# Two SwiGLU networks in one kernel: the first chunk's product taken before the norm's roots are known

## What is computed

```python
def rms_norm(x, g, eps=NORM_EPS):
    xf = x.astype(jnp.float32)
    y = xf * lax.rsqrt(jnp.mean(xf * xf, axis=-1, keepdims=True) + eps)
    return (y * g.astype(jnp.float32)).astype(x.dtype)

def swiglu_ffn(h, norm, w13, w2):
    u = rms_norm(h, norm) @ w13
    return (jax.nn.silu(u[..., :FFN_HIDDEN]) * u[..., FFN_HIDDEN:]) @ w2
```

## Time and profile before

| | |
|---|---|
| median of 3 runs | 3366.26 us (3365.47 to 3368.86) |
| the profiled execution's own time | 3368.29 us |
| span of its trace | 3366.4 us |
| TensorE busy | 3304.4 us, 98% of the span |
| VectorE busy | 1763.8 us, 52% |
| GpSimd, ScalarE busy | 1492.0 us, 44%; 1435.9 us, 43% |
| granted TensorE clock, mean | 0.997 |

### The profile page before, as it was taken

One profiled execution on the slowest core, in us unless ns is written; L12 is line 12 of the kernel. 1 busy time (PEld: TensorE's weight loads), 2 busy tenths in 40 slices (PEclk: granted clock), 3 DMA queues, 4 the chain that ended last, 5 costly groups with the idle time before them and its releaser, 6 DMA issues. The chain is left out here.

```text
span 3366.4 us, 48377 instructions
## 1 busy us (share of the span) xinstructions
PE 3304.4 (98%) x19096; PEld 2724.3 (81%) x19096; DVE 1763.8 (52%) x3073; ACT 1435.9 (43%) x2918; POOL 1492.0 (44%) x1353
## 2 busy tenths in 40 slices
PE   9999999999998999999999999999999999999999
PEld 7769788888886788888888877888888877888887
DVE  4765675636456664656353376445153186545143
ACT  4662354323355554532333337344343246444343
POOL 3330254454443545354544443445554443444543
PEclk9999999999999999999999999999999999999999
DMA  4210024545221123354533220232323220123331
GB/s 124 75 57 4 27 88 151 194 144 192 85 88 51 42 97 100 101 169 163 170 125 117 82 77 11 75 100 86 102 85 103 92 82 26 51 89 99 100 94 56
DMA packets 233851, 317.79 MB, mean 94 GB/s; under 512 B 8877, under 2 KB 151196, under 8 KB 233628
## 3 DMA queue, kind: packets, MB, share of 16 engines
q1 hardware_dynamic: 204982, 260.50, 24.1%
q10 hardware_dynamic: 28646, 54.22, 4.7%
HBM read 312.59 MB, written 2.10 MB: 93 GB/s over the span
## 5 line engine op out<-in xcount | busy, mean ns | idle before, releaser
L417 PE MATMUL banks<-split,split 128*128 128x512 f32 (+2 forms) x11760 | 2675.2, 388 | 8.1 <-ACT split L436 3.7
L417 PEld LDWEIGHTS banks<-split,split 128*128 128x128 f32 x11760 | 2183.7, 188 | 476.5 <-issue 15.7
L440 POOL TENSOR_TENSOR split<-kept,split 128x512 fp32r<-128x512 f32 (+3 forms) x1174 | 1363.8, 1166 | 1581.1 <-ACT split L436 1578.6
L436 ACT ACTIVATE split<-kept 128x512 fp32r<-128x512 f32 (+3 forms) x1174 | 648.9, 559 | 1436.4 <-PE banks L417 1389.3
L2047 DVE SCALAR_TENSOR_TENSOR work<-banks,kept,work 128x511 f32<-128x511 f32 (+1 forms) x176 | 120.4, 745 | 257.1 <-ACT work L2029 256.3
L1044 DVE SCALAR_TENSOR_TENSOR work<-work,kept 128x512 f32<-128x512 f32 x168 | 195.5, 1164 | 6.0
L989 DVE SCALAR_TENSOR_TENSOR kept<-banks,kept 128x512 f32<-128x512 f32 (+1 forms) x56 | 34.3, 669 | 207.8 <-PE banks L417 207.8
L987 DVE TENSOR_TENSOR kept<-banks,kept 128x512 f32<-128x512 f32 (+1 forms) x72 | 41.1, 625 | 193.2 <-PE banks L417 193.2
L613 DVE COPY work<-banks 128x512 f32<-128x512 f32 (+1 forms) x64 | 37.4, 643 | 187.9 <-PE banks L417 187.9
L1986 DVE TENSOR_TENSOR work<-work,banks 128x512 f32<-128x512 f32 x44 | 28.3, 684 | 165.5 <-ACT work L1974 165.5
L1673 ACT ACTIVATE work<-work 128x128 f32<-128x128 f32 (+3 forms) x160 | 89.5, 560 | 47.0 <-DVE work L1733 46.1
(11 more groups left out here) (460 smaller groups left out, 3106.7 us busy)
## 6 DMA issues: line engine op xcount, KB each, us to landing
work<-in_mod_w ACTq DMA_DIRECT2D x48, 1024.0 KB, 6.5
kept<-in_ffn_w SPq DMA_DIRECT2D x94, 512.0 KB, 4.9
kept<-in_w_up SPq DMA_DIRECT2D x88, 512.0 KB, 4.7
kept<-in_w_in SPq DMA_DIRECT2D x36, 1024.0 KB, 5.0
kept<-in_od_w_in SPq DMA_DIRECT2D x19, 1024.0 KB, 5.2
kept<-in_ffn_w SPq DMA_DIRECT2D x18, 1024.0 KB, 5.4
kept<-in_w_down SPq DMA_DIRECT2D x18, 1024.0 KB, 5.2
kept<-in_ev_w_in SPq DMA_DIRECT2D x8, 1024.0 KB, 5.2
```

Of the source, the lines that this page charges most:

```text
L417: m = pe.matmul(self.bank(q, j), lhs, rhs, start=t == 0 and i == 0, stop=t == job.KT - 1 and i == 2)
L436: act.activation(self.weights(s, 0), self.source(s), ACT.Copy).then_inc(self.rounded, 1)
L440: pool.tensor_tensor(self.weights(s, 1), self.source(s), self.weights(s, 0), ALU.subtract).then_inc(self.k.slices_split, 1)
```

## The change

The norm in front of `up0` becomes a `RawFirst`, in both layers. While `xo` is added chunk by chunk, x times gain is split without the roots (L926 and L930 of the changed kernel). Chunk 0 of `up0` is multiplied from these raw halves directly behind `xo`; the sum of squares and the spreading of the roots are put on TensorE behind slices 1 and 3 of that chunk. ScalarE copies the spread roots from their bank to SBUF (L967). VectorE multiplies the four finished banks of chunk 0 by the roots in place (`even_out`, L594), and makes the normed halves for the later chunks during chunk 0 (L956, L946, L950), in the same buffers as the raw ones. The last chunk of `xo` isn't rushed any more, all 8 squares are folded on VectorE (two more L724), and the `keep_busy` matmuls, the sums of L715 and the early table load (L978) are gone.

```diff
@@ Stream @@
+            high, low = finish.operands(c, hi, lo)
+            terms = (whi, high(t)), (wlo, high(t)), (whi, low(t))
@@ Finish @@
+        elif c == 1 and self.raw_first():
+            self.after.await_normed_high(pe, t)
...
+    def operands(self, c, hi, lo):
+        return self.after.raw if c == 0 and self.raw_first() else (hi, lo)
+
+    def even_out(self, dve, q, j):
+        bank = self.stream.bank(q, j)
+        self.stream.await_tile(dve, q, j)
+        if j == 0:
+            dve.wait_ge(self.after.kept, 1)
+        dve.tensor_tensor(bank, bank, self.after.row, ALU.mult).then_inc(self.after.evened, 1)
@@ @@
+class RawFirst(Rms):
+    SUM, ROOT, SPREAD, SCALE = 1, 1, 3, 4
...
+    def round(self, act, t):
+        act.activation(self.raw[0](t), self.src(t), ACT.Identity, scale=self.gain(t)).then_inc(self.rounded, 1)
+
+    def rest(self, dve, t):
+        dve.wait_ge(self.rounded, t + 1)
+        dve.scalar_tensor_tensor(out=self.raw[1](t), in0=self.src(t), scalar=self.gain(t), in1=self.raw[0](t), op0=ALU.mult,
+                                 op1=ALU.subtract).then_inc(self.halved, 1)
...
+    def beside(self, pe, t):
+        if t == self.SUM:
+            self.sum_folded(pe, self.k.PS[:, self.bank_at, :])
+        if t == self.SPREAD:
+            self.spread_roots(pe, self.k.PS[:, self.bank_at + 1, :])
...
+    def normed_scale(self, dve, t):
+        self.stream.await_slice(dve, self.slice0 + t)
+        if t >= self.n_tmp:
+            dve.wait_ge(self.halved, self.T + t - self.n_tmp + 1)
+        dve.scalar_tensor_tensor(out=self.tmp(t % self.n_tmp), in0=self.src(t), scalar=self.gain(t), in1=self.row,
+                                 op0=ALU.mult, op1=ALU.mult).then_inc(self.scaled, 1)
...
+    def vector_beside(self, dve, link):
+        for _ in range(self.slice0):
+            yield
+        for i in range(self.SCALE + self.T // 2 + 1):
+            if i == self.ROOT:
+                self.roots(dve, link)
+            if i == self.SCALE:
+                dve.wait_ge(self.kept, 1)
+            for t in range(2 * (i - self.SCALE), 2 * (i - self.SCALE + 1)):
+                if 0 <= t < self.T:
+                    self.normed_scale(dve, t)
+                if 1 <= t <= self.T:
+                    self.normed_rest(dve, t - 1)
+            yield
@@ AddToX: scalar, and vector alike @@
+        if self.raw:
+            for j in range(self.job.tiles(c)):
+                self.rms.round(act, self.first(c) + j)
+                yield
@@ Gated @@
     def tensor(self, pe, c, t):
+        if c == 0 and self.raw_first():
+            self.after.beside(pe, t)
...
     def vector(self, dve, link, q, c):
+        if c == 0 and self.raw_first():
+            for j in range(4):
+                self.even_out(dve, q, j)
+            yield
```

More of the change, by code:

```diff
@@ L358, in __init__, with free_banks @@
             self.done_by.append(whole)
+    def free_banks(self, job):
+        last = self.first_chunk(job) + len(job.widths) - 1
+        assert job.tiles(len(job.widths) - 1) <= 2
+        return self.groups[last] * 4 + 2
     def first_chunk(self, job):
@@ L872, in finish_vector, with __init__, signals, used_by @@
         yield
+class RawFirst(Rms):
+    SUM, ROOT, SPREAD, SCALE = 1, 1, 3, 4
+    def __init__(self, k, T, src, gain, halves, squares_at, n_squares, rows_at, tmp, n_tmp, dim, raw=None):
+        super().__init__(k, T, src, gain, halves, squares_at, n_squares, rows_at, tmp, n_tmp, dim)
+        self.raw = raw or halves
+        self.row = self.sq[:, n_squares - 1, :]
+    def signals(self, st):
+        super().signals(st)
+        self.kept, self.evened = st.signals(2)
+    def round(self, act, t):
[4 more added lines that the diff above has]
+                                 op1=ALU.subtract).then_inc(self.halved, 1)
+    def used_by(self, stream, job, bank):
+        self.stream, self.bank_at = stream, bank
+        self.slice0 = next(s for s, one in enumerate(stream.slices) if one[1] is job)
+    def beside(self, pe, t):
[3 more added lines that the diff above has]
+            self.spread_roots(pe, self.k.PS[:, self.bank_at + 1, :])
+    def normed_round(self, act, t):
+        act.wait_ge(self.scaled, t + 1)
+        act.activation(self.hi(t), self.tmp(t % self.n_tmp), ACT.Copy).then_inc(self.rounded, 1)
+    def normed_rest(self, dve, t):
+        dve.wait_ge(self.rounded, self.T + t + 1)
+        dve.tensor_tensor(self.lo(t), self.tmp(t % self.n_tmp), self.hi(t), ALU.subtract).then_inc(self.halved, 1)
+    def normed_scale(self, dve, t):
[4 more added lines that the diff above has]
+                                 op0=ALU.mult, op1=ALU.mult).then_inc(self.scaled, 1)
+    def scalar_beside(self, act):
+        for _ in range(self.slice0):
+            yield
+        for i in range(self.SCALE + self.T // 2 + 1):
+            if i == self.ROOT:
+                self.root_of(act)
+            if i == self.SPREAD:
+                act.wait_ge(self.spread, 1)
+                act.activation(self.row, self.rows, ACT.Copy).then_inc(self.kept, 1)
+            for t in range(2 * (i - self.SCALE), min(2 * (i - self.SCALE + 1), self.T)):
+                if t >= 0:
+                    self.normed_round(act, t)
+            yield
+    def vector_beside(self, dve, link):
+        for _ in range(self.slice0):
+            yield
+        for i in range(self.SCALE + self.T // 2 + 1):
+            if i == self.ROOT:
+                self.roots(dve, link)
[7 more added lines that the diff above has]
+            yield
+    def await_normed_high(self, eng, t):
+        eng.wait_ge(self.rounded, self.T + t + 1)
+    def await_normed_half(self, eng, t):
+        eng.wait_ge(self.halved, self.T + t + 1)
@@ new lines, with __init__, signals, scalar @@
+class Besides(Part):
+    def __init__(self, norms):
+        self.norms = norms
+    def signals(self, st):
+        pass
+    def scalar(self, act, q, c):
+        works = [norm.scalar_beside(act) for norm in self.norms]
+        while any([next(work, 0) is None for work in works]):
+            yield
+    def vector(self, dve, link, q, c):
+        works = [norm.vector_beside(dve, link) for norm in self.norms]
+        while any([next(work, 0) is None for work in works]):
+            yield
+    def more(self, block):
+        pass
@@ L946, in tensor_end @@
             self.rms.sums_bank = self.sums_bank()
-        elif self.rms:
+        elif self.rms and not self.raw:
             q2 = self.stream.first_chunk(self.job) + 2
@@ L976, in scalar @@
             yield from self.rms.finish_scalar(act)
[L977 removed]
+        if self.rms and self.rms.by_halves and c == len(self.job.widths) - 2:
             act.activation(self.k.idle, self.k.ones[:, 0:1], ACT.Sqrt)
@@ L996, in vector @@
                 yield
+        if self.raw:
+            for j in range(self.job.tiles(c)):
+                self.rms.rest(dve, self.first(c) + j)
+                yield
         if self.rider and c == 0:
             yield from self.rider.vector(dve, link, self.RIDES, self.k.PS[:, q % 2 * 4, :])
-        if self.rms and c == len(self.job.widths) - 1:
+        if self.rms and not self.raw and c == len(self.job.widths) - 1:
             yield from self.rms.finish_vector(dve, link)
@@ L2113, in scalar, with tensor @@
                 yield
+    def tensor(self, pe, c, t):
+        if c == 0 and self.raw_first():
+            self.after.beside(pe, t)
     def vector(self, dve, link, q, c):
+        if c == 0 and self.raw_first():
+            for j in range(4):
+                self.even_out(dve, q, j)
+            yield
         for lag in range(1, 4):
```

47 lines of the change are left out of this document (34 added, 13 removed).

## The result

The changed kernel takes 3382.28 us (median of 4 runs, 3380.53 to 3382.56), the kernel before 3366.45 on the same chip: 15.8 us slower, ratio 1.0043, 95% interval 1.0031 to 1.0056 (the ratios, here and below, compare all runs, and lie up to 0.05% from those of the medians). The direction was forecast; the size was not, +8.8 us, and the time lies 0.8 us above the range.

What follows compares the result with a forecast made beforehand. TensorE, busy 98% of the span, was taken as the bound. Per network -4.6 + 2.3 + 5.2 = +2.9 us, +5.8 for both, plus 3.0 for the clock: +8.8, 3375.1 us, range 3366.5 to 3381.5.

Steps and rivals of the forecast that it cites:

- The gap: TensorE between `xo` and `up0`: 6.02 us go away, 1.4 come back inside chunk 0, net -4.6 us per network.
- The early waits: TensorE waits around the start of `up0` because VectorE's raw rests delay additions and folds: 2.3 us per network.
- The late wait: TensorE waits in front of the transposes of the rider's sum, because VectorE has more work after chunk 0: 5.2 us per network.
- three terms: Parts of the wait at the rider's transposes: late first product 1.5, five VectorE instructions 3.1, extra GpSimd hits 0.6 us.
- The five instructions: VectorE's two scalings and three rests for tiles 5 to 7, between chunk 0's end and the rider's end: 3.1 us.
- The first term: First product behind chunk 0 comes 1.5 us late, as VectorE enters late and does four `even_out` first.
- The clock: TensorE's clock falls to half in the new empty waits: 1.5 us each, 3.0 for both networks, between 0 and 7.
- A: Rival, won after all: VectorE keeps up, wait at the transposes under 2.3 us, time 3357.1 to 3361.7; chance 0.05.
- B: Rival: TensorE waits as worked out but the clock holds or falls inside the wait, -1 to +6.7 us; chance 0.34.
- C: The forecast itself, waits and clock: +6.7 to +15 us, 3373 to 3381; chance 0.54.
- D: Rival, more loss: early waits at their ceiling or half clock lasts, 3381 to 3388 us; chance 0.07.

Runs made afterwards that it cites:

- e6_rests: Changed kernel with raw rests of tiles 2 to 7 put behind the next additions or last folds, sum behind slice 2, spreading behind slice 4: 3375.62 us.
- e7_both: Changed kernel with riders moved away from chunk 0, raw rests put behind the additions, sum and spreading one slice later: 3360.07 us, ratio 0.9979.
- e2_one: The change made in the first of the two networks only, the second as in the kernel before: 3373.87 us, ratio 1.0021.
- e4_late: Changed kernel with the transposes of chunk 0's rider two slices later, behind slice 7 of chunk 1 rather than slice 5: 3369.83 us, ratio 1.0006.
- e8_dose: Kernel before with five more VectorE instructions, result unused, behind chunk 0's second products in both networks: 3378.18 us, ratio 1.0030.
- e1_fill: Changed kernel with 20 filling matmuls on TensorE in front of the transposes of chunk 0's rider: 3376.29 us, ratio 1.0022.

## Why the prediction came out so

**The gap**, -4.6 us: right. Gone are 6.02, back come 0.92 + 0.35 = 1.3.

**The early waits**, 2.3 us: right in size (2.2) and kind. 0.33 us for GpSimd's half of a slice and 1.18 for the fold show as idle time; most of the rest is in the row of 100 matmuls, which takes 23.15 us where 22.8 would do, and at the edges of the two waits. `e6_rests` and `e7_both` move the rests behind the additions, and the sum and the spreading one slice later; they show no early wait. How much of that is due to either move was not separated.

**The late wait**, 5.2 us: right in size, 5.3. What it rests on was shown by the dose: in the kernel before, each VectorE instruction more makes TensorE wait 0.6 us, with hits that move but don't add up; five and ten lie on one line through zero, and fewer than five were not tried. The forecast wait had three terms, 1.5, 3.1 and 0.6 us. The five instructions took 3.1 (557.27 to 559.80, and 0.60 for the third rest), and what VectorE lost to hits from L2156 to the rider's end was 4.7 us, where it had been 4.1. The first term had only half of the cause. I had the first product 1.5 us late because VectorE enters late and has the four `even_out` to do first. It was late by 1.6 (556.07 is 4.3 us behind the end of chunk 0, at 540.76 + 48 x 0.229 = 551.8, as against 2.75), and the four did end only 0.13 us ahead of it, but without them it was as late. ScalarE is behind as well, since tile 5's rounding, which waits for the scaling, stands in front of its table load, and that scaling was hit (1.78 us). I had counted ScalarE as in time.

**The clock**, 3.0 us: the mechanism was right and the size too small. It fell in both networks and cost 2.7 + 2.3 = 5.0; filling the wait gave that back. I had weighted a fall that passes while TensorE is idle. The trace shows that it isn't over then: clock 0.50 from within the wait to 5.7 us behind its end. The rule of the Trainium skill ("TensorE: Matmul & The Clock Gate", Part 1), by which I cited the clock as a cost of the empty wait, held. In the traces of these kernels all nine empty waits of 5.3 us and more had a clock of 0.50 behind them, and the filled ones had 1.00.

**The sum.** The networks cost 2 x 2.8 + 5.0, by the distances 10.5 us, where 8.8 were forecast; the term that was too small is the clock. The further 3.3 us of mixer and stretch have no term in the forecast at all. They are falls of the clock in stages with short matmuls, which the change doesn't touch. A last 1.8 us comes from the step to the median: the forecast carried a difference of profiled executions over to it, but those are 14.0 us apart (3382.25 and 3368.29) and the medians 15.8. With both the time passes the range; the networks alone would have left it inside.

In `e2_one` the falls of mixer and stretch were about as much (3.6 us) for half of the change, and `e7_both` met such falls too (5.7 us) while its networks won 10. Why these kernels met more of them than the profiled execution of before is open: the work just before the falls is the same, so it isn't that, and I made no kernel that only shifts those stages in time. Two facts narrow it. When a kernel comes to the stretch doesn't sort them: `e4_late` gets there 0.6 us earlier than the kernel before and loses 1.6 us in it, `e8_dose` gets there 5.5 us later and loses nothing. And executions of one program differ: 23 runs of the kernel before go from 3365.9 us, at a mean granted clock of 0.998, to 3371.8, at 0.996.

**The rivals.** A, won after all, fell by its own test (the wait was 5.3, not under 2.3). B, waits without the clock, is `e1_fill`'s network part, 5.5 us, and not what the changed kernel does. C had the mechanism, with its clock too small, but the time lies above its bounds, in those of D. Of D's two causes the early waits were not at their ceiling; half clock did last longer than taken (5.0 us for 3.0), and the rest is falls elsewhere, which no rival named.

## What to carry to other kernels

A row that shows no wait is no sign of slack: where a consumer arrives within 0.1 us of its input, work moved to the producer's engine is paid in full by the consumer, here 0.6 us for an instruction of 0.6. When serial work is taken out of a gap and spread over the next stage, look at that stage's last deadline first (here the rider), move that as well, and the gap's time stays won: moving the rider alone left -2.7 us a network, moving the rests alone +2.8 and +3.9, both together -5.0. If a stall can't be avoided, an idle TensorE costs more than one that is filled: waits of 5.3 us drew 1.5 to 2.7 us behind them.

## What the runs showed of the hardware

- How long TensorE idled and whether the clock fell: 0.8 us, in neither network (`e1_fill`); 1.8 us, in one of two (`e4_late`); 3.0, in one of two (`e8_dose`); 5.3 and 6.1 to 6.3, each of nine times. A fall behind such a wait cost between 1.3 us (`e6_rests`, first network) and 2.7. Among short matmuls the same idle time of 0.95 us had a fall behind it in one trace and none in another.
- The product of a bank with an SBUF tile, written back to the bank, took 2.48 us for four, 0.62 each, no slower than the products of the earlier trace rows that write SBUF (1.28 for two). GpSimd's split from 554.20 to 555.49 lay inside these and cost them nothing.
- In the stretch between the second products and the rider's end GpSimd split four slices, and VectorE lost 4.1 us to them in the kernel before, 4.2 with five instructions more and 4.4 with ten more. Which instructions were hit changed, the sum hardly.
